# Making constants beside the first projection, and loading the parameter vectors behind the first norm

## The reference

```
u = rmsnorm(h, norm_mix_g[l]) @ w_in[l]
o_sb = sb_group(u[..., :SB_IN], sb_out_g[l])
o_rw = rwkv7_group(u[..., SB_IN:], shift_mu[l], rw_w0[l], rw_w2[l], rw_a0[l], rw_a2[l], ...)
h = h + jnp.concatenate([o_sb, o_rw], axis=-1) @ w_out[l]
xn = rmsnorm(h, norm_ffn_g[l]).reshape(B * S, D)
y = hier_moe(xn, ...)
```

## Time and profile before

| | us |
|---|---|
| median of three runs | 1682.17 |
| the three runs | 1678.59, 1687.53, 1682.17 |
| the profiled execution | 1687.3 |
| its span | 1685.6 |
| PE busy in the span | 1399.6 (83%) |
| DVE, ACT, POOL busy | 423.6, 354.1, 157.2 |

### The profile page before, as it was taken

The page is one execution under the profiler, slowest core; times in us unless marked ns, Lnnn a source line. Parts: engine busy times, 40 slices in busy tenths (PEclk is TensorE's granted clock), DMA queues, the critical chain, the costliest instruction groups (busy, mean ns, idle before and its releaser), DMA issues. The chain is left out here.

```text
span 1685.6 us, 23511 instructions
## 1 busy us (share of the span) xinstructions
PE 1399.6 (83%) x9945; PEld 702.9 (42%) x9945; DVE 423.6 (25%) x826; ACT 354.1 (21%) x615; POOL 157.2 (9%) x215
## 2 busy tenths in 40 slices
PE   2989998877797888877279999577889799999991
PEld 2434444577545433322034444465545433333320
DVE  2223505432213211100420100592512311111103
ACT  1023016443121111100211100322522011111011
POOL 4000002254000000100100000240000000000001
PEclk9989999999996998998689999786999599999995
DMA  5021100200145799999433210001152388998954
GB/s 188 21 80 50 50 0 0 101 3 4 56 177 199 279 418 419 419 417 398 169 108 125 75 51 0 1 1 38 64 193 112 135 331 327 362 363 342 362 210 169
DMA packets 70007, 287.34 MB, mean 170 GB/s; under 512 B 11475, under 2 KB 12570, under 8 KB 57634
## 3 DMA queue, kind: packets, MB, share of 16 engines
q1 hardware_dynamic: 57072, 250.41, 38.1%
q0 software_dynamic: 6400, 16.79, 3.0%
q10 hardware_dynamic: 6450, 18.92, 2.9%
HBM read 269.30 MB, written 23.07 MB: 173 GB/s over the span
## 5 line engine op out<-in xcount | busy, mean ns | idle before, releaser
L323 PE MATMUL banks<-mixT,ring 128*128 128x512 f32 x672 | 295.9, 603 | 6.7 <-DVE mixT L301 6.7
L323 PEld LDWEIGHTS banks<-mixT,ring 128*128 128x128 f32 x672 | 129.9, 194 | 172.4 <-issue 165.2
L1873 PE MATMUL banks<-arena_moe,mixT 128*32 128x512 f32 x768 | 172.1, 597 | 0.0
L1323 PE MATMUL banks<-ring,mixT 128*128 128x512 f32 x256 | 115.3, 611 | 8.4 <-PEq L51 8.4
L1873 PE MATMUL banks<-ring,mixT 128*32 128x512 f32 x768 | 115.6, 610 | 5.0 <-DMA arena_moe<-in_w_up 4.1
L1509 POOL DMA_INDIRECT arena_moe<-normed_rows,arena_moe x32 | 33.3, 1040 | 745.5 <-DVE arena_moe L1537 605.2
L1700 PE MATMUL banks<-arena_moe,mixT 128*64 128x512 f32 x256 | 67.8, 688 | 35.4 <-DMA arena_moe<-in_exp_w_up 35.4
L320 PE MATMUL banks<-ring,mixT 128*128 128x512 f32 x192 | 82.9, 592 | 0.0
L1323 PEld LDWEIGHTS banks<-ring,mixT 128*128 128x128 f32 x256 | 49.7, 196 | 70.6 <-issue 70.6
L1873 PEld LDWEIGHTS banks<-ring,mixT 128*32 128x32 f32 x768 | 32.7, 113 | 85.5 <-issue 85.5
L1700 PE MATMUL banks<-ring,mixT 128*64 128x512 f32 x256 | 60.0, 623 | 9.5 <-DMA ring<-in_exp_w_up 8.2
(11 more groups left out here) (384 smaller groups left out, 1927.5 us busy)
## 6 DMA issues: line engine op xcount, KB each, us to landing
ring<-in_w_in SPq DMA_DIRECT2D x18, 1024.0 KB, 7.4
arena_moe<-in_exp_w_gate SPq DMA_DIRECT2D x16, 1024.0 KB, 15.7
arena_moe<-in_exp_w_up SPq DMA_DIRECT2D x16, 1024.0 KB, 20.0
arena_moe<-in_exp_w_down SPq DMA_DIRECT2D x16, 1024.0 KB, 22.4
ring<-in_exp_w_gate SPq DMA_DIRECT2D x16, 1024.0 KB, 16.9
ring<-in_exp_w_up SPq DMA_DIRECT2D x16, 1024.0 KB, 18.5
ring<-in_exp_w_down SPq DMA_DIRECT2D x16, 1024.0 KB, 23.1
arena_moe<-in_w_gate SPq DMA_DIRECT2D x8, 2048.0 KB, 10.6
```

The source lines that it names most:

```text
L323: last = pe.matmul(bank[:], w[:, c, i * P:(i + 1) * P], m.mixT[:, c, :], start=(c == 0), stop=(c == DC - 1))
L1323: last = pe.matmul(m.banks[k % 3][:], m.mixT[:, c, i * P:(i + 1) * P], w[:, c, :], start=(c == 0), stop=(c == DC - 1))
L1873: last = pe.matmul(hb[u][T * i:T * (i + 1), :], z.xe[:, j, at:at + T], both[:, :, j, half * 256:half * 256 + 256], start=(j == 0), stop=(j ...
```

## The change

The phase `setup_phase` and its barrier are gone; its parts go into the block of `phase_project1`. SP loads the first gain alone (`norm_mix_g`, 8 rows) ahead of x, and the low-rank weights directly behind the ring items. Each x tile has its own semaphore. TensorE waits for the identity and the gain, transposes the gain into bank 6, and DVE copies it. The norm is `norm_first_dve` and `norm_first_pe`: DVE scales tile t and then takes tile t - 1, and six banks are used in turn. ACT issues the other 14 vector loads and the two permuted ones behind its part of the norm. TensorE waits for these 14 and transposes them into bank 7, ahead of the first projection; DVE copies them and makes `centre` there. POOL makes the identity first, then fills, then `same64`, and the rest of the constants after; `small` gives a semaphore three times (after the first zeroing, after `same64`, at the end). ACT waits for the third before its take of chunk 14, TensorE for the second before L548.

```diff
+def load_gain(sp, m, io, x, ph):
+    sp.dma_start(x.raw_gain[:], io["norm_mix_g"].rearrange("l (c p) -> (l c) p", p=P)).then_inc(ph.sem("gain"), 16)
...
+    g.link(pool.memset(m.ident[:], 0.0))
+    pool.affine_select(out=m.ident[:], in_=m.ident[:], compare_op=ALU.not_equal, fill=1.0, base=0,
+                       pattern=[[-1, P]], channel_multiplier=1).then_inc(ph.sem("ident"), 1)
+    pool.memset(m.small[:, 16:], 0.0).then_inc(ph.sem("small"), 1)
...
+def norm_first_pe(pe, ph, m, scaled):
+
+    for t in range(NT):
+        pe.wait_ge(ph.sem("scaled"), t + 1)
+        for half in range(2):
+            k = 2 * t + half
+            if k >= 6:
+                pe.wait_ge(ph.sem("normed"), k - 5)
+            for j in range(4):
+                c = 4 * half + j
+                last = pe.transpose(m.banks[k % 6][:, j * P:(j + 1) * P], scaled[:, t, c * P:(c + 1) * P], m.ident[:])
+            last.then_inc(ph.sem("turned"), 1)
...
+    scale(0)
+    v.wait()
+    for t in range(1, NT):
+        scale(t)
+        taken(t - 1)
+    taken(NT - 1)
...
         def _(sp):
+            load_gain(sp, m, io, x, ph)
+            load_first(sp, m, io, x, ph)
             sp.dma_start(x.lw[0:64, :], io["rw_w2"][0]).then_inc(ph.sem("low"), 16)
...
-            norm_act(act, ph, m, x.rows, x.scaled, lambda e, t: e.wait_ge(ph.sem("rows"), 64))
+            norm_act(act, ph, m, x.rows, x.scaled, lambda e, t: e.wait_ge(ph.sem(f"rows{t}"), 16))
+            load_vectors_act(act, m, io, x, ph)
...
-            norm_scale_dve(dve, ph, m, x.rows, x.scaled, v)
-            norm_gain_dve(dve, ph, m, COLUMN["norm_mix_g"])
+            dve.wait_ge(ph.sem("gain_turned"), 1)
+            v.mark(dve.tensor_copy(m.params[:, 0:GAIN_ROWS], m.banks[6][:, 0:GAIN_ROWS]))
+            norm_first_dve(dve, ph, m, x.rows, x.scaled, COLUMN["norm_mix_g"], v)
+            dve.wait_ge(ph.sem("vectors_turned"), 1)
+            v.mark(dve.tensor_copy(m.params[:, GAIN_ROWS:NVEC], m.banks[7][:, 0:NVEC - GAIN_ROWS]))
+            dve.wait_ge(ph.sem("small"), 2)
+            v.link(dve.tensor_scalar(m.centre[:], m.same64[:], -1.0 / 64, None, ALU.mult))
+            v.link(dve.tensor_tensor(m.centre[:], m.centre[:], m.ident[:], ALU.add))
...
-            norm_turn_pe(pe, ph, m, x.scaled)
+            pe.wait_ge(ph.sem("ident"), 1)
+            pe.wait_ge(ph.sem("gain"), 16)
+            pe.transpose(m.banks[6][:, 0:GAIN_ROWS], x.raw_gain[:], m.ident[0:GAIN_ROWS, 0:GAIN_ROWS]).then_inc(ph.sem("gain_turned"), 1)
+            norm_first_pe(pe, ph, m, x.scaled)
+            pe.wait_ge(ph.sem("vectors"), 16 * len(VECTORS))
+            pe.transpose(m.banks[7][:, 0:NVEC - GAIN_ROWS], x.raw[0:NVEC - GAIN_ROWS, :],
+                         m.ident[0:NVEC - GAIN_ROWS, 0:NVEC - GAIN_ROWS]).then_inc(ph.sem("vectors_turned"), 1)
             pe.wait_ge(ph.sem("normed"), NORMED)
```

More of the change, by code:

```diff
@@ L149 @@
 PERMUTED = {"norm_ffn_g": NVEC, "ffn_norm_2": NVEC + 8}
[L152 to L246, removed]
@@ new lines, with load_vectors_act @@
+GAIN_ROWS = 8
+def load_gain(sp, m, io, x, ph):
+    sp.dma_start(x.raw_gain[:], io["norm_mix_g"].rearrange("l (c p) -> (l c) p", p=P)).then_inc(ph.sem("gain"), 16)
+def load_vectors_act(act, m, io, x, ph):
+    for name, n in VECTORS[1:]:
+        src = io[name]
+        c = COLUMN[name] - GAIN_ROWS
+        if name == "fox_norm_2":
+            for half in range(2):
+                act.dma_start(x.raw[c:c + 1, 64 * half:64 * half + 64], src).then_inc(ph.sem("vectors"), 16)
+            continue
+        if len(src.shape) == 3:
+            src = src.rearrange("l h d -> l (h d)")
+        act.dma_start(x.raw[c:c + n, :], src.rearrange("l (c p) -> (l c) p", p=P)).then_inc(ph.sem("vectors"), 16)
+    for name, c in PERMUTED.items():
+        act.dma_start(m.params[:, c:c + DC], io[name].rearrange("l (p c) -> (l p) c", c=DC)).then_inc(ph.sem("permuted"), 16)
@@ L306, with norm_first_dve, scale, taken @@
 NORMED = 2 * NT
+def norm_first_pe(pe, ph, m, scaled):
+    for t in range(NT):
+        pe.wait_ge(ph.sem("scaled"), t + 1)
+        for half in range(2):
+            k = 2 * t + half
[5 more added lines that the diff above has]
+            last.then_inc(ph.sem("turned"), 1)
+def norm_first_dve(dve, ph, m, rows, scaled, gain, v):
+    def scale(t):
+        inverse_rms_dve(dve, ph, m, t, v)
+        dve.tensor_scalar(scaled[:, t, :], rows[:, t, :], m.small[:, 12 + t:13 + t], None, ALU.mult).then_inc(ph.sem("scaled"), 1)
+    def taken(t):
+        for half in range(2):
+            k = 2 * t + half
+            dve.wait_ge(ph.sem("turned"), k + 1)
+            g = m.params[:, gain + 4 * half:gain + 4 * half + 4].unsqueeze(2).broadcast_to([P, 4, P])
+            dve.tensor_tensor(m.mixT[:, 4 * half:4 * half + 4, t * P:(t + 1) * P],
+                              m.banks[k % 6][:].rearrange("p (a b) -> p a b", b=P), g,
+                              ALU.mult).then_inc(ph.sem("normed"), 1)
+    scale(0)
[4 more added lines that the diff above has]
+    taken(NT - 1)
 def project_pe(pe, ph, m, n, cols, chunks, first, ring_count, rows_form):
@@ L2591, in two_blocks_kernel @@
         x = Mix1(m)
-        ahead = {n: nc.alloc_semaphore(f"first_{n}") for n in ("rows", "ring0", "ring1")}
-        setup_phase(nc, m, io, lambda sp: load_first(sp, m, io, x, ahead))
         g2s, _ = m.view(m.arena_size - HW, HW)
-        phase_project1(nc, m, io, g2s, ahead)
+        phase_project1(nc, m, io, x, g2s)
         phase_stick(nc, m, x)
```

69 lines of the change are left out of this document (63 added, 6 removed).

## The result

The changed kernel takes 1669.97 us, the median of six runs (1667.18 to 1672.91). Six runs of the kernel before, taken beside them, have a median of 1681.63 (1678.59 to 1687.53). The medians differ by 11.7 us. The ratio, which is taken over all runs and not from the two medians, is 0.992, with an interval of 0.990 to 0.994; on 1682 us that is a gain of 13.5, between 10 and 17. The forecast was 1670.4, a gain of 11.8 us. The profiled execution of the changed kernel took 1672.01, its span is 1670.3.

A forecast was written before the change was run, and what follows sets the result against it. The 37.4 us before the first projection, held by POOL's constants and then the norm, were taken as the bound; starting at 25.1 saves 12.3, less 0.5 for the clock: 11.8, so 1670.4 us, range 1662.5 to 1677.5.

The forecast's parts named there:

- signs for being wrong: Idle before projection ended by DVE's gain, start after 30, wide scales much over 0.76, or a later stage's clock changed.
- Cause and gate: Before the first projection: POOL's constants and the barrier held the norm; afterwards TensorE's wait for 14 vector loads gates it.
- The first scaled tile: Norm's start: x lands at 4.8, then the old chain of 4.94 us, table load included, gives 9.7.
- The last root: ACT's last square root in the interleaved norm, at about 15.55; ACT free for vector loads at 16.2.
- Contention: POOL's constants beside DVE's norm: three wide scales each lose half a POOL instruction, 0.65 us, bounds 0 to 4.3.
- The second rival: POOL holds DVE up at each norm step: 4.3 us instead of 0.65, time 1674.1; chance 0.12.
- The issues: ACT's 14 vector loads after the norm: last starts 5.44 us after 16.2, at 21.65; bounds 4.3 and 12.5.
- The landing: Last vector load, from issue to landing: 3.0 us, at 24.65; bounds 2.3 and 7.1.
- Transpose and hand-over: TensorE's transpose of the landed vectors before the first projection: 0.45 us, so the projection starts at 25.1.
- Clock: TensorE at the projection's start, after longer idleness: 0.5 us more than before, bounds 0 and 1.5.
- Hidden at no cost: Vectors' copy, centre instructions, permuted loads, POOL's later constants and SP's low-rank loads delay nothing in the first phase.
- the clock rival: Later stages shifted by 12 us: one falls to 1.2 GHz, adding 54 us, time 1724; chance 0.04.

The follow-up runs named there:

- the gate put back: Changed kernel with TensorE also waiting for POOL's last constant before the gain's transpose: 1679.64 us, ratio 0.9967 to the kernel before.
- its removal: Changed kernel with TensorE's wait for the vector loads and their transpose moved behind the projection's first chunk: 1662.38 us; repeated on another chip, 1661.17 us.
- the fillers: Changed kernel with five extra thrown-away products in TensorE's wait for the vectors: 1668.0 us, ratio 0.9908 to the kernel before.
- POOL behind the norm: Changed kernel with POOL waiting for the norm's end after its first fills, before the remaining constants: 1671.4 us, ratio 0.9913 to the kernel before.
- the two without it: Changed kernel with second weight item and low-rank loads held until the vectors' transpose, 1662.43 us; changed kernel with TensorE waiting for all constants, 1679.64 us.
- the five executions of the table: Profiled spans: kernel before 1685.6; changed kernel 1670.3 and 1665.4; changed kernel with vectors' wait behind the first chunk 1657.0, with TensorE awaiting all constants 1680.0 us.

## Why the prediction came out right, step by step

The time, 1669.97, is 0.4 us from the forecast; by the ratio the gain is 13.5 and not 11.8. The mechanism held too. But two terms of the sum were missed by over 2 us each, in opposite directions, so the closeness is in part luck. Of the signs that the prediction names for being right, the start near 25 (24.34) and the vectors' loads as what ends the wait came true; the last root near 16 and the end of the norm near 20 came 2 us earlier (14.10 and 17.80). One of its signs for being wrong showed too, a wide scale much over 0.76, but in one of four (1.20).

**Cause and gate: right.** The constants set the old start, as the gate put back shows (34.88), and the new gate is the vector load, as its removal shows (18.12).

**The first scaled tile: forecast 9.7, measured 8.77.** The step charged the 4.94 us of before with its table load of 1.28 in the path. The row at 0.82 decides the point that I left between 0 and 1.28: the load stands ahead of the wait for x and hides. A second load, for the root, remains in the chain at 5.84. It was inside the 4.94 of before as well. The Trainium skill ("ScalarE: Activation LUTs", section "What ACT_TABLE_LOAD costs") gives 1283 ns for the load and about 1380 more for a drain, 2.66 in all for a switch to another set. The first number agrees. Of the drain this trace shows nothing ahead of the root, which starts at 7.14, 1.30 behind the start of the load.

**The last root: forecast 15.55 and ACT free at 16.2, measured 14.10 and 14.11.** Of these 2.1 us the hidden table load gives 1.28 and the earlier x 0.1. The contention came to 0.45 up to there instead of 0.65, which gives 0.2. The rest, 0.5, is the interleaved chain: 14.10 - 8.77 = 5.33, contention in the second scale included, against 5.85 forecast without any. That the interleaving by itself brings nothing held: from the first scaled tile to the end of the norm 9.03, against 9.4 forecast and 9.3 before.

**Contention: a right mechanism, and near the right size.** 0.45 us up to the last root where 0.65 was forecast, 0.7 over all four scales. The prediction weighed a rule of the Trainium skill ("SBUF — State Buffer", section "Who interferes with whom"). The trace agrees in what stretches: the wide scales beside POOL, POOL's fills beside them, and not the instructions of one column. That the one blocks the other for its whole length this trace doesn't show: the first scale started at 7.57, when POOL's selection of 1.09 us from 7.14 had 0.66 to go, and lost 0.44. The second rival had priced all ten DVE instructions alike, at 4.3 us; it is refuted by the 0.45.

**The issues: forecast 5.44, measured 18.88 - 14.11 = 4.77.** The good end of the bounds, 4.3, was closer. The last issue thus came 2.8 earlier than forecast, at 18.88 and not 21.65.

**The landing: forecast 3.0, measured 5.2. This is the term that was most wrong, though inside its bounds of 2.3 and 7.1.** The prediction took a value near the quiet row because at 21.65 the stream "has little left". The issue came at 18.88, in its midst, and four executions with the stream in that place (two of the changed kernel, the fillers, POOL behind the norm) landed the load after 4.9 to 5.4 us, the two without it after 1.3. So the two misses hang together: an earlier issue meets more of the stream. The sum should have priced the landing by the stream at the hour of the issue, and that hour was itself uncertain by what the table load, the contention and the issues left open. Whether an issue at 21.65 would also have landed near 24 is not shown. The load waits before its packet moves, as the packets above show; why it waits they don't say. The Trainium skill ("DMA: Bandwidth & Descriptors", section "Queues, rings and completion order") says that a DMA engine alternates, packet by packet, between the queues for which it has work; by that a small load passes the stream instead of waiting for its end. The trace agrees behind 17.5 us, when ACT's packets move beside SP's; but for over 3 us before that none had moved, with loads already issued (the first at 14.11), and for that the section has no number.

**Transpose and hand-over: forecast 0.45, measured 0.29.** Start forecast 25.1, measured 24.34.

**Clock: forecast 0.5, measured 1.1.** The ten chunks took 1.14 more than before. It is inside the bounds of 0 and 1.5. The reason given was more idleness ahead. There was more (7 us in one wait, and gaps of up to 1.5 us between the tiles before it), and with the gaps filled the clock stayed up; but the fall came ahead of the wait, so the gaps have a part in it that the prediction didn't see. Sum of the start: 13.06 - 1.14 = 11.9 against 11.8.

**Hidden at no cost: right.** The vectors' copy and the centre instructions end at 25.13; no later idle time in the first phase is ended by POOL. What lies behind the first phase is the same work, and nothing was found for the clock rival, 1724. The first two stages of the earlier trace rows, 12 to 14 us earlier in the changed kernel, are at the levels of before:

```profile
328.00:428.00 100.00, 78.00 (x3199) 73.36 (x3198) 28.11 (x58) 33.59 (x59) 37.84 (x45) 1.00 0.02 4
1126.00:1146.00 20.00, 20.00 (x96) 20.00 (x95) 0.00 (x0) 3.26 (x6) 0.00 (x0) 0.50 0.00 1
```

**Left open.** Why the clock's share in the later phases, above all the last, differs from one execution to the next. It does so in both kernels and in the experiments, and no run here was made for it. Nor is it known where the gain lies that the gate on the constants leaves in the total beyond this stage.

## What to carry to other kernels

Work that is taken off the start of a chain exposes the next latest input, so list all inputs of the first useful instruction with the times at which they land, and put every wait behind the first work that doesn't need it: here one wait moved behind one chunk was worth 6.3 us at the end of ten chunks, on top of the 11.9 of the change. A small load issued beside a saturated stream must be costed as such a load beside such a stream (here 5 us), not by what it takes alone (1.3); hold back the part of the stream that isn't needed yet, or issue the small one first. And when a forecast hits, look at the terms before believing it.

## What the hardware showed that I had not expected

- From issue to landing a load of 0.2 KB took 1.3 us on idle DMA engines (twice) and 5.2 beside the weight stream, although the two are in different queues. Some 4 of the 5.2 us lie ahead of its packet, which moved in 0.04.
- Behind short transposes with gaps of up to 1.5 us TensorE's clock fell to 1.2 GHz at 16.0 us, ahead of the wait of 7 us, and at 18.0 in another execution of the same kernel. With the gaps filled it stayed at 2.4 GHz, and so it did in single executions with 4.56 us of thrown-away products within the wait and with the vectors issued first.
- The profile's clock reads 1.00 as long as TensorE has hardly worked, and says nothing there: the first 16 transposes took 3.67 us (8.83 to 12.50), 0.23 each, and the 8 from 12.86 on 1.09, 0.14 each, both at a clock shown as 1.00.
- The clock's first cold stretch is worth 2.0 to 2.6 us of the stage, but neither that nor a norm that ends 1 us earlier could be found in the total, where single phases scatter by more (the last one by 7.3 us in the five executions of the table).
